# First weight of experts 16 to 25 as one 8 MB transfer each, in a mixture-of-experts block on one Trainium2 core

## The reference, cut to what matters

```python
h2 = rms_norm(x, norm2_gain[layer])
logits = h2 @ w_router + b_router                   # top 4 of 32, softmax over them -> combine
for e in range(32):
    z = einsum('bsd,df->bsf', h2, w1[e]) + b1[e]    # w1[e]: 1024 x 2048
    glu = minimum(z[..., 0::2], 7); lin = clip(z[..., 1::2], -7, 7)
    act = glu * sigmoid(1.702 * glu) * (lin + 1)
    out = out + combine[..., e:e+1] * (einsum('bsf,fd->bsd', act, w2[e]) + b2[e])   # w2[e]: 1024 x 1024
x = x + out;  return rms_norm(x, final_gain)
```

## Time and profile before

| | us |
|---|---|
| median of 3 runs | 1082.29 (1081.51 to 1082.70) |
| profiled execution | 1082.48 |
| its span | 1080.7 |
| TensorE busy in the span | 1039.1 (96%) |
| TensorE weight load busy | 400.2 (37%) |
| VectorE, ScalarE busy | 302.9 (28%), 157.1 (15%) |
| moved by DMA | 429.79 MB (millions of bytes), 398 GB/s over the span |

### The profile page before, as it was taken

How to read it: one execution, slowest core, us unless ns; L and a number is a source line. 1 busy time by engine, 2 the same in 40 slices (tenths; PEclk the granted TensorE clock), 3 DMA queues, 4 the chain that set the end, 5 groups by cost and what they waited for, 6 DMA issues and landing times.

```text
span 1080.7 us, 11540 instructions
## 1 busy us (share of the span) xinstructions
PE 1039.1 (96%) x4616; PEld 400.2 (37%) x4616; DVE 302.9 (28%) x704; ACT 157.1 (15%) x282; POOL 22.5 (2%) x29
## 2 busy tenths in 40 slices
PE   8999999999999999899998999898989899999997
PEld 7458454333333333233333333233333233333332
DVE  2455622422222222132221222221323222221231
ACT  1231333110101111101010111011101101111112
POOL 1212000000000000000000000000000000000000
PEclk9999999999999999999998999999999999999999
DMA  9886947999999999999999999999999999999995
GB/s 326 241 245 268 379 176 317 384 432 412 431 431 431 431 428 432 434 429 431 428 429 431 435 430 428 434 433 432 429 433 433 432 429 434 432 432 431 425 429 230
DMA packets 33050, 429.79 MB, mean 398 GB/s; under 512 B 4892, under 2 KB 6336, under 8 KB 16352
## 3 DMA queue, kind: packets, MB, share of 16 engines
q1 hardware_dynamic: 31104, 426.03, 93.6%
q10 hardware_dynamic: 1216, 1.70, 1.1%
q0 software_dynamic: 704, 1.71, 0.6%
HBM read 426.80 MB, written 2.62 MB: 397 GB/s over the span
## 4 chain that ended last, share of the span: by engine, by line
PE 70%; DMA 27%; DVE 1%; SPq 1%; issue 1%; ACT 0%; DVEq 0%
PE ps L1361 31%; DMA w1r<-w_mlp 22%; PE ps L1389 13%; PE ps L1430 5%; PE ps L1110 4%; PE ps L1339 3%; PE ps L1098 3%; DMA w2r<-w_mlp 2%; DMA w1r<-w_out 1%; PE ps L1157 1%; PE ps L1263 1%; PE ps L1232 1%; PE ps L1403 1%; DMA w1r<-w_in 1%; PE ps L1347 1%; PE ps L1369 1%
## 5 line engine op out<-in xcount | busy, mean ns | idle before, releaser
L1361 PE MATMUL ps<-w1r,arena 128*64 128x512 f32 x2040 | 484.9, 611 | 22.4 <-DMA w1r<-w_mlp 22.0
L1361 PEld LDWEIGHTS ps<-w1r,arena 128*64 128x64 f32 x2040 | 141.8, 139 | 285.8 <-issue 279.6
L1389 PE MATMUL ps<-w2r,arena 128*64 128x512 f32 x960 | 212.0, 593 | 7.3 <-DMA w2r<-w_mlp 7.3
L1389 PEld LDWEIGHTS ps<-w2r,arena 128*64 128x64 f32 x960 | 68.0, 137 | 147.1 <-issue 131.4
L981 DVE TENSOR_TENSOR acc<-ps,acc 128x512 f32<-128x512 f32 x56 | 36.1, 686 | 175.1 <-PE ps L1430 175.1
L973 DVE TENSOR_TENSOR arena<-arena 128x512 f32<-128x512 f32 x32 | 22.2, 692 | 163.5 <-ACT arena L593 163.4
L935 DVE TENSOR_TENSOR arena<-ps,cols 128x512 f32<-128x512 f32 x31 | 21.4, 692 | 139.3 <-PE ps L1347 139.3
L597 ACT ACTIVATE arena<-ps 128x512 f32<-128x512 f32 x31 | 18.5, 597 | 288.4 <-PE ps L1369 288.3
L1339 PE MATMUL ps<-h,arena 128*64 128x512 f32 x248 | 58.7, 592 | 0.0
L602 ACT ACTIVATE arena<-ps 64x512 f32<-64x512 f32 x29 | 17.2, 592 | 269.5 <-PE ps L1389 269.5
L1430 PE MATMUL ps<-arena 128*128 128x512 f32 x112 | 55.5, 618 | 0.0
(11 more groups left out here) (257 smaller groups left out, 579.4 us busy)
## 6 DMA issues: line engine op xcount, KB each, us to landing
w1r<-w_mlp SPq DMA_DIRECT2D x54, 4096.0 KB, 30.9
w2r<-w_mlp SPq DMA_DIRECT2D x32, 2048.0 KB, 18.7
w2r<-w_mlp SPq DMA_DIRECT2D x14, 4096.0 KB, 20.8
w1r<-w_mlp SPq DMA_DIRECT2D x17, 2048.0 KB, 10.3
w1r<-w_in SPq DMA_DIRECT2D x7, 2048.0 KB, 17.1
w1r<-w_mlp SPq DMA_DIRECT2D x12, 1024.0 KB, 8.3
w1r<-w_out SPq DMA_DIRECT2D x2, 2048.0 KB, 13.7
rel_table<-arena ACTq DMA_DIRECT2D x1, 1536.0 KB
```

The lines of the kernel that those rows point to most:

```text
L1361: ins = mm(ps[64 * c:64 * c + 64, 2 * par + n, :], hgT[:, par, k % 4, 64 * (k // 4):64 * (k // 4) + 64], cols_z, start=False, stop=(k == 7))
L1389: ins = mm(ps[at:at + 64, 4 + c, :], actT[:, k % 4, 64 * (k // 4):64 * (k // 4) + 64], w2r[:, k // 2, col:col + 512], start=(k == 0), stop ...
```

## The change

Three things change together.

1. The layout: feature 8p + 4c + j is now on partition p in row 4c + j. All of a partition's eight rows of w1 are then one contiguous run of 64 KB in memory, and a half of w1 is 128 runs of 32 KB that begin 64 KB apart. The pieces of experts 0 to 3 and 31 keep runs of 16 or 8 KB, which now begin 64 KB apart too. `copy_half` reads the activations with a step of 8 elements in place of 4, out of the whole row in place of one half of it; `gain_q` follows.
2. Experts 16 to 25: w1 is issued as one transfer of 8 MB (`next_w1_whole`), which waits until all eight rows of expert e-2 are released, and lands on the first half's semaphore. TensorE waits for it at k = 0 and has no wait at k = 4.
3. The loops are cut to fit: SyncE's are partly written out, TensorE's second loop over pairs of experts becomes two (experts 16 to 25, 26 to 29).

```diff
-        w1_v = w_mlp1[0].rearrange("e (c p i a) f -> e c i p (a f)", c=2, p=P, i=2)
-        w1_c = w_mlp1[0].rearrange("e (c p j) f -> e c p (j f)", c=2, p=P)
+        w1_v = w_mlp1[0].rearrange("e (p c i a) f -> e c i p (a f)", c=2, p=P, i=2)
+        w1_c = w_mlp1[0].rearrange("e (p c j) f -> e c p (j f)", c=2, p=P)
+        w1_p = w_mlp1[0].rearrange("e (p j) f -> e p (j f)", p=P)
...
+            def next_w1_whole(base, e, par):
+                sp.wait_ge(w1_used, 8 * base + (8 * (e - 2) + 8))
+                sp.dma_start(w1r[:, 8 * par:8 * par + 8, :].rearrange("p a f -> p (a f)"), w1_p[e]).then_inc(w1_half[2 * par], 16)
...
-                with sp.Fori(6, 8) as m:
-                    ahead(2 * m - 1, 2 * m + 1, 1)
-                    ahead(2 * m, 2 * m + 2, 0)
-                with sp.Fori(8, NE // 2 - 1) as m:
-                    ahead(2 * m - 1, 2 * m + 1, 1, next_w2_whole)
-                    ahead(2 * m, 2 * m + 2, 0, next_w2_whole)
+                ahead(11, 13, 1)
+                ahead(12, 14, 0)
+                ahead(13, 15, 1)
+                next_w2(base, 14)
+                next_w1_whole(base, 16, 0)
+                with sp.Fori(8, 12) as m:
+                    next_w2_whole(base, 2 * m - 1)
+                    next_w1_whole(base, 2 * m + 1, 1)
+                    next_w2_whole(base, 2 * m)
+                    next_w1_whole(base, 2 * m + 2, 0)
+                next_w2_whole(base, 23)
+                next_w1_whole(base, 25, 1)
+                for e in range(24, 29):
+                    ahead(e, e + 2, e % 2, next_w2_whole)
...
-            pool.dma_start(gain_q, norm2_gain[0].rearrange("(c q j) -> q c j", c=2, q=P)).then_inc(gq_in, 16)
+            pool.dma_start(gain_q, norm2_gain[0].rearrange("(q c j) -> q c j", c=2, q=P)).then_inc(gq_in, 16)
...
-                                     acc[:, t, 512 * c:512 * c + 512].rearrange("p (q j) -> p j q", j=4), ACT.Copy).then_inc(h2_ready, 1)
+                                     acc[:, t, :].rearrange("p (q c j) -> p c j q", c=2, j=4)[:, c], ACT.Copy).then_inc(h2_ready, 1)
...
-                if halves and k % 4 == 0:
-                    pe.wait_ge(w1_half[2 * par + k // 4], 16 * lap)
+                if halves and k == 0:
+                    pe.wait_ge(w1_half[2 * par], 16 * lap)
+                if halves and k == 4 and late is not None:
+                    pe.wait_ge(w1_half[2 * par + 1], 16 * late)
...
-                with pe.Fori(8, NE // 2 - 1) as m:
-                    step(base, hb, wb, rb, m, 0, whole=True)
-                    step(base, hb, wb, rb, m, 1, whole=True)
+                gone = WHOLE_PAIRS[1] - WHOLE_PAIRS[0]
+                with pe.Fori(*WHOLE_PAIRS) as m:
+                    step(base, hb, wb, rb, m, 0, whole=True, gone=None)
+                    step(base, hb, wb, rb, m, 1, whole=True, gone=None)
+                with pe.Fori(WHOLE_PAIRS[1], NE // 2 - 1) as m:
+                    step(base, hb, wb, rb, m, 0, whole=True, gone=gone)
+                    step(base, hb, wb, rb, m, 1, whole=True, gone=gone)
```

More of the change, by code:

```diff
@@ L34 @@
 WHOLE = (15, 29)
+WHOLE_PAIRS = (8, 13)
 SWEEPS = S // SLOTS
@@ L1348, in gather_T, with z_rows @@
                 ins.then_inc(hg_tr, 1)
-            def z_rows(base, lap, k, par, halves, early=None, row=None):
-                if halves and k % 4 == 0:
-                    pe.wait_ge(w1_half[2 * par + k // 4], 16 * lap)
+            def z_rows(base, lap, k, par, halves, early=None, row=None, late=None):
+                if halves and k == 0:
+                    pe.wait_ge(w1_half[2 * par], 16 * lap)
+                if halves and k == 4 and late is not None:
+                    pe.wait_ge(w1_half[2 * par + 1], 16 * late)
                 if not halves and k % 2 == 0:
@@ L1458, in gates_T, with step @@
                 ins.then_inc(gT_tr, 1)
-            def step(base, hb, wb, rb, m, par, first=False, last=False, whole=False):
+            def step(base, hb, wb, rb, m, par, first=False, last=False, whole=False, gone=0):
                 e = 2 * m + par
@@ L1464, in step @@
                     lap = rb * (HALVES - par) + m - 1
+                    late = None if gone is None else rb * (HALVES - par - WHOLE_PAIRS[1] + WHOLE_PAIRS[0]) + m - 1 - gone
                 else:
                     lap = rb * (2 + par) + m + 1
+                    late = None
                 head = first and par == 0
@@ L1486, in step @@
                     gather_T(base, e + 1)
-                z_rows(base, lap, 4, par, halves)
+                z_rows(base, lap, 4, par, halves, late=late)
                 if par == 1 and not first:
@@ L1564, in sweep @@
                     step(base, hb, wb, rb, m, 1)
-                with pe.Fori(8, NE // 2 - 1) as m:
-                    step(base, hb, wb, rb, m, 0, whole=True)
-                    step(base, hb, wb, rb, m, 1, whole=True)
+                gone = WHOLE_PAIRS[1] - WHOLE_PAIRS[0]
[5 more added lines that the diff above has]
+                    step(base, hb, wb, rb, m, 1, whole=True, gone=gone)
                 late = wb - (WHOLE[1] - WHOLE[0])
-                step(base, hb, late, rb, NE // 2 - 1, 0, last=True)
+                step(base, hb, late, rb, NE // 2 - 1, 0, last=True, gone=gone)
                 final(base, hb, late, rb)
```

## The result

The changed kernel takes 1105.94 us (median of 3 runs, 1105.29 to 1106.70) against 1082.29; the ratio is 1.0214, 95% interval 1.0197 to 1.0230. The forecast was 1106.5, range 1097 to 1117. Its profiled span is 1104.1 us, 23.4 more than before.

A forecast was written before the change was run, and what follows sets the result against it. The stream of weights, at 432 GB/s, was taken as the bound. A first loss of 3.9 us plus four pairs at 5.0 (20.1) gave 24.0 on the profiled 1082.48: forecast 1106.5 us, range 1097 to 1117.

The forecast's parts named there:

- The stream of weights sets the pace, and the wait takes the cover away: Experts 16 to 25: weights pace the kernel; late odd steps let the stream run dry, 5.0 us lost per repeating pair.
- A19: Time when all of expert 19's w1 has landed (A plus expert number): forecast 700.8, before 696.9, so 3.9 us lost.
- The clock, 2.65 us a step: Odd steps after some 7 us of TensorE idling: first 16 matmuls lose 2.65 us, bounds 1.7 and 3.4.
- The restart, 2.4 us on top of the bytes: Each restart of the stopped weight stream, five times: 2.4 us on top of the bytes, bounds 1.0 and 4.0.
- An even step has no stop: Even steps, some 25 us long, end before the next odd w1 lands, so the stream goes on; nothing lost.
- The layout, the copy, the gain, the written-out code at nothing: Remaining edits: spaced runs, `copy_half` step of 8, gain transfer, extra loop code; taken as 0, copy bounds 0 and 2.2 us.
- 0.1 us an expert from the longer runs: 64 KB runs in whole w1 transfers save 0.1 us an expert, bounds 0 and 0.13; 29.03 us for w2 and w1.
- Faster by fewer transfers: Rival, chance 0.02: each transfer costs its own 2.4 us even in a full queue; 10 fewer save 24 us, time 1058.
- TensorE as the bound: Rival, chance 0.02: TensorE, 96% busy, bounds the kernel and w1 has landed whole before each step; no change, 1082.
- Slower spaced runs: Rival, chance 0.03: halves of experts 4 to 15 and 26 to 30 read at 325 GB/s; 109 us more, 1215.
- Cheap clock and restart: Rival, chance 0.05: cold clock and stream restart cost almost nothing; 1.0 us lost a pair, 5 in all, 1087.5.
- Runs of 64 KB cut into pieces of 32 KB: Possibility inside the forecast, no chance given: cutting takes back the 0.1 us an expert, 0.7 us on the path.

The follow-up runs named there:

- e1: Changed kernel's layout alone: every w1 from expert 4 on still comes in two halves with two waits; 1082.41 us, 0.9996 of the kernel before.
- e2: Changed kernel, but w1 of experts 16 to 25 issued in halves, both awaited before the up-projection's first row; 1105.88 us, 1.0212 of the kernel before.
- e4: Changed kernel with only odd experts 17 to 25 whole and awaited whole, even ones in halves; 1106.55 us, 1.0224 of the kernel before.
- e8: Changed kernel, steps 16 to 25 shortened (scatter 64, down-projection 256 of 512 columns), filler matmuls before each; 1082.41 us, 0.9995 of the kernel before.
- e5: Changed kernel plus 31 unused bf16 matmuls after each even step 16 to 24; 1101.31 us, 1.0164 of the kernel before.
- e6: Changed kernel with scatter matmuls of odd steps 17 to 25 covering 64 of 512 columns; 1094.12 us, 1.0103 of the kernel before.
- e7: Changed kernel with experts 26 to 29 whole too; 1118.16 us, 1.0329 of the kernel before.
- e3: Changed kernel with only even experts 16 to 24 whole and awaited whole, odd ones in halves; 1092.17 us, 1.0078 of the kernel before.
- e10: Changed kernel with only even experts 16 to 24 whole, plus 16 unused bf16 matmuls before each of their steps; 1085.18 us, 1.0025 of the kernel before.

## Why the prediction was right, step by step

- **The stream of weights sets the pace, and the wait takes the cover away.** Right. e1 and e2 show that the wait alone makes the loss, e4 that the odd steps make it, e8 that it vanishes when the steps are short enough.
- **The times.** Step 16 was forecast to start at 609.5 and started at 609.89; its end 636.4, measured 636.97; step 17's start 638.6, measured 639.16; its end 669.4, measured 669.93; A19 700.8, measured 701.38. A27 was forecast at 954.4. The issue of line 310 at 922.3 landed 32.0 us later, at 954.3.

```profile
DMA to landing us min/median/max: 22.7/27.3/32.0
```

- **The clock, 2.65 us a step.** A little too much: the first 16 matmuls of steps 19, 21, 23 and 25 lost 1.45, 2.67, 1.65 and 3.00 us against 3.65, on average 2.19. The bounds 1.7 and 3.4 nearly held. The forecast was 0.5 us a pair too high, 1.8 us in all.
- **The restart, 2.4 us on top of the bytes.** Cost plus cover is 2.3, 2.6, 2.5 and 2.3 us in steps 17, 19, 21 and 23. The last, step 25, had 3.7, so that over the five the term was 1.4 us too small. That the errors of clock and restart nearly cancel is luck: the sum is closer than its terms. The 2.0 us of the Trainium skill (DMA: Bandwidth & Descriptors, Anatomy of one DMA), which the prediction sets beside its 2.4, is a fit for transfers issued from GpSimd; these are issued from SyncE. Why the last restart is dearer is open. It is so in every kernel that stops there and goes over to other loops at expert 26 (3.7 in e2 and e4, 4.0 in e5 and e6), and not in e7, where the loops run on and the restart at the same cover (-3.0) cost 5.3 and not 6.6. The halves are not the reason (e2). In 900 to 960 the changed kernel's trace has one 16 KB transfer of instructions on another queue, of 1 us, 14 us after TensorE has entered its added loop; e7, which has no such loop, has none there. That this is the cause is argued, not shown. The rows of queues there, of the changed kernel and of e7:

```profile
q1 hardware_dynamic: 799, 23.56, 92.0%
q8 instruction: 1, 0.02, 0.1%
```

```profile
q1 hardware_dynamic: 543, 23.53, 91.9%
```

- **An even step has no stop.** Right in the sum, but for a reason that was too simple. Step 16 ended 2.1 us before A17 and by the forecast cost nothing; w1 of 18 came 1.6 us late. That was hidden, because step 17 ended later still. With the rule of the forecast (in time if 1 us before the end) e3 and e6 were missed by 10 and 12 us.
- **The layout, the copy, the gain, the written-out code at nothing.** Right as a sum (e1); none of them was run alone.
- **0.1 us an expert from the longer runs.** In the changed kernel pairs of landings without a stop are 29.05 us apart (701.38 to 730.43), before 29.14. Right, and too small to matter.
- **The rivals.** Faster by fewer transfers: excluded by e2 against the changed kernel, 1105.88 us with ten transfers more against 1105.94, where 20 to 24 us were at stake. TensorE as the bound: excluded, since its waits before steps 17 to 25 were ended by w1. Slower spaced runs: excluded by e1. Cheap clock and restart: excluded by the rows above. Runs of 64 KB cut into pieces of 32 KB: the trace has 1280 packets of 64 KB (ten experts of 128), of 2.4 us each, so they are not cut.

## What to carry to other kernels

When a stream of transfers sets the pace, ask of each wait on it what its end will issue, and how much is still queued then. The wait for a larger piece cost no transfer time here; it cost the queue's cover, and once that is gone, every microsecond of the waiting engine's step is paid in full. Here a pair's odd step was 29.07 us long against 29.13 us of queued transfers, near enough that only the details (0.14 us to start, 1 us for data to flow, a cold clock) decided, and all of them pointed the same way.

## What the runs showed of the hardware that was not expected

- A queue must be refilled well before it is empty. With 5.9 us or more of transfers queued (2.5 million bytes at 432 GB/s) an issue costs nothing in nearly all cases; with 3.3 to 5.5 us up to 0.9; with 2 to 3 us anything from 0 to 2.9; on an empty queue 2.3 to 2.8 and the gap (3.7 to 4.0 at step 25). Exceptions at covers of 6.8 to 12.3 us: 0.4 in the kernel before, 0.2 in e4, 0.7 in e3, 0.8 in e8, twice 1.2 in e10. Each had a 16 KB transfer of instructions between issue and landing, but so had issues that lost nothing (step 26 of e1); whether that is the cause was not tested.
- The last landing is not the moment at which the queue runs dry. The packets of the changed kernel's trace show that at the end of step 17 the first of the 16 engines ran out at 667.5 and the 15th at 668.1, where w1 landed at 669.75; the issue at 669.93 had its first packet at 670.9. In e3, with an issue at 754.16, 2.6 us before the landing, 11 of the 16 engines stood still at 755.0, 0.8 us after the issue, and some of them until 758.2; that issue cost 2.9 us. In all traces some engine ran out at every issue with less than 4.5 us of cover, and at none with 5.9 or more. This is part of the cost and not all: averaged over the 16 engines the standing still at covers of 2 to 3 us is 0.2 to 1.5 us, and the packets there also took longer, by 0.4 to 1.2 us in sum for each engine, where it is 0.0 to 0.2 at long covers. So in e3 the DMA share stayed at 0.99 while the rate was 418 GB/s. Why they take longer, and why the engines end so far apart, stays open.
- One transfer of 8 MB in 64 KB runs, or two of 4 MB in 32 KB runs, back to back in a full queue: the same to 0.1 us in 29.
- After 7 us of waiting the granted clock cost the next step 1.45 to 3.0 us, hardly more than after 2.3 us (1.70). Filling the wait with matmuls whose result isn't used takes it away.
